# Second attention: column sides in turn for the value products, and forget-gate terms in bias tables

## The reference, cut to what matters

```python
def fox_mixer(cols, q_g, k_g, forget_bias):
    q = rms_norm(to_heads(cols['c_q'], FOX_HEADS), q_g)
    k = rms_norm(to_heads(cols['c_k'], FOX_HEADS), k_g)
    v = to_heads(cols['c_v'], FOX_HEADS)
    log_f = jax.nn.log_sigmoid((cols['c_f'] + forget_bias).astype(jnp.float32))
    c = jnp.cumsum(log_f, axis=1).transpose(0, 2, 1)
    ...
        logits = (jnp.einsum('bhqd,bhsd->bhqs', qi, k).astype(jnp.float32) * (HEAD_DIM ** -0.5)
                  + ci[..., None] - c[:, :, None, :])
        logits = jnp.where(t_pos[:, None] >= key_pos[None, :], logits, NEG_INF)
        probs = jax.nn.softmax(logits, axis=-1)
        return jnp.einsum('bhqs,bhsd->bhqd', probs.astype(v.dtype), v)
```

## Time and profile before

| | us |
|---|---|
| median of 3 runs | 2215.01 |
| the runs | 2211.79, 2215.01, 2215.42 |
| profiled execution, its span | 2214.5 |
| PE busy in it | 2169.7 (98%) |
| VectorE busy in it | 1212.5 (55%) |
| ScalarE busy in it | 519.1 (23%) |

### The profile page before, as it was taken

How to read it: one execution, slowest core, us unless ns; L and a number is a source line. 1 busy time by engine, 2 the same in 40 slices (tenths; PEclk the granted TensorE clock), 3 DMA queues, 4 the chain that set the end, 5 groups by cost and what they waited for, 6 DMA issues and landing times.

```text
span 2214.5 us, 40429 instructions
## 1 busy us (share of the span) xinstructions
PE 2169.7 (98%) x17748; PEld 1767.9 (80%) x17748; DVE 1212.5 (55%) x2285; ACT 519.1 (23%) x1103; POOL 159.8 (7%) x180
## 2 busy tenths in 40 slices
PE   8999899999999999999999999999999999999999
PEld 5854689994688888885666667899988877789999
DVE  4647744444545555755645554487544353228874
ACT  3224722221100000004434443100121143302100
POOL 0002132220000000000211221000010000000000
PEclk9999999999999999999999999999999799999999
DMA  7221022221322245323212221545454422144453
GB/s 314 96 76 57 20 80 80 80 80 39 111 80 95 79 190 226 116 101 138 86 58 76 76 77 58 190 172 180 172 183 160 152 77 96 66 153 146 169 174 132
DMA packets 38247, 260.70 MB, mean 118 GB/s; under 512 B 4647, under 2 KB 6327, under 8 KB 7480
## 3 DMA queue, kind: packets, MB, share of 16 engines
q1 hardware_dynamic: 34416, 248.83, 31.1%
q10 hardware_dynamic: 2760, 6.11, 0.7%
q0 software_dynamic: 896, 3.18, 0.4%
HBM read 256.49 MB, written 1.08 MB: 116 GB/s over the span
## 4 chain that ended last, share of the span: by engine, by line
PE 85%; DVE 3%; ACT 1%; issue 1%; POOL 0%; ACTq 0%; DVEq 0%; POOLq 0%
PE pairs L315 24%; PE bank L315 11%; PE pairs L1804 11%; PE pairs L185 11%; PE bank L1375 4%; PE pairs L1375 4%; PE pairs L2785 4%; PE pairs L1933 1%; PE bank L439 1%; PE pairs L2739 1%; PE bank L1907 1%; PE bank L453 1%; PE bank L1897 1%; PE bank L2719 1%; PE bank L1872 1%
## 5 line engine op out<-in xcount | busy, mean ns | idle before, releaser
L1804 PE MATMUL pairs<-h_sb,ring_sb 128*128 128x512 f32 (+1 forms) x784 | 263.9, 492 | 0.0
L1804 PEld LDWEIGHTS pairs<-h_sb,ring_sb 128*128 128x128 f32 x784 | 147.5, 190 | 105.3 <-issue 94.7
L185 PE MATMUL pairs<-h_sb,ring_sb 128*128 128x256 f32 (+1 forms) x720 | 223.4, 470 | 0.9 <-DVE h_sb L669 0.9
L185 PEld LDWEIGHTS pairs<-h_sb,ring_sb 128*128 128x128 f32 x720 | 136.9, 192 | 84.7 <-issue 72.3
L315 PE MATMUL pairs<-mid 128*128 128x128 f32 (+1 forms) x1304 | 197.3, 306 | 0.6 <-DVE mid L357 0.6
L315 PEld LDWEIGHTS pairs<-mid 128*128 128x128 f32 x1304 | 179.5, 192 | 11.2 <-issue 1.1
L335 DVE TENSOR_TENSOR mid<-ring_sb 128x512 f32<-128x512 f32 (+1 forms) x105 | 71.7, 683 | 123.7 <-DMA ring_sb<-weights 69.4
L315 PE MATMUL bank<-mid 128*128 128x256 f32 x544 | 122.7, 380 | 0.1
L315 PE MATMUL pairs<-h_sb,ring_sb 128*128 128x128 f32 (+1 forms) x784 | 118.2, 303 | 3.0 <-ACT h_sb L583 2.3
L185 PE MATMUL pairs<-big,ring_sb 128*128 128x256 f32 (+1 forms) x544 | 114.2, 376 | 0.5 <-DVE big L2848 0.5
L315 PEld LDWEIGHTS pairs<-h_sb,ring_sb 128*128 128x128 f32 x784 | 106.1, 194 | 10.3 <-ACT h_sb L583 2.7
(11 more groups left out here) (529 smaller groups left out, 3649.0 us busy)
## 6 DMA issues: line engine op xcount, KB each, us to landing
ring_sb<-weights SPq DMA_DIRECT2D x237, 1024.0 KB, 4.8
x_sb<-tokens ACTq DMA_DIRECT2D x1, 2048.0 KB, 12.1
mid<-bias_table POOLq DMA_DIRECT2D x1, 1536.0 KB, 9.0
const_table<-consts ACTq DMA_DIRECT2D x1, 1200.0 KB, 10.6
mid<-bias_table POOLq DMA_DIRECT2D x1, 1024.0 KB, 12.4
out<-x_sb ACTq DMA_DIRECT2D x4, 256.0 KB, 2.6
lora_w<-lora ACTq DMA_DIRECT2D x1, 512.0 KB, 14.0
vec_table<-vectors SPq DMA_DIRECT2D x1, 285.0 KB, 16.1
```

Of the source, the lines that this page charges most:

```text
L185: last = pe.matmul(out, w[:, k, c, :], rhs(j * kt + k), start=(j == 0 and k == 0), stop=(j * kt + k == k_end - 1))
L1804: ins = pe.matmul(m.pairs[:, at % 2, c, 0:T], w[:, k, c, :], m.h[:, k, TOK - T:TOK], start=(k == 0), stop=(k == 7))
```

## The change

Value products have the side as the inner loop now: each product of side 0 is followed by the same product of side 1. The fox scores are the query-key products alone, as in swa. For each fox head h there are two bias tables (in columns of `x` and `h` that are free by then), one for each query tile. They are built during earlier units: after the values of the units with chunk 0 to 7 (nsa1 and swa), PE broadcasts the row of `logf` of head h = chunk to all partitions, into the other half of that chunk's PSUM bank (`forget_row_pe`); VectorE adds to it the query's own sum, a column of `forget_tok`, and the causal mask (`forget_bias_dve`), before it copies the unit's heads out. `forget_tok` comes from two more small products in group 9 of the projection, which now waits for the second count of `gates_moved`, and one more copy on VectorE in group 11.

```diff
@@ -2383,8 +2383,10 @@
             v_turn_pe(s, m, g - 7)
         if g == 9:
             pe.wait_ge(sem["v_tokens"], s.next("v_tokens"))
-            pe.wait_ge(sem["gates_moved"], s.next("gates_moved"))
+            pe.wait_ge(sem["gates_moved"], s.next("gates_moved", 2))
             for tt in range(2):
+                pe.matmul(m.bank[:, 3, 8 * tt:8 * tt + 8], m.c2[CF, 28, tt * P:tt * P + P], m.const("ident")[CF, CF],
+                          start=True, stop=True)
                 ins = pe.transpose(m.bank[:, 2, 24 * tt:24 * tt + 24], m.gate_rows[:, tt * P:tt * P + P],
                                    m.const("ident")[0:24, 0:24])
             ins.then_inc(sem["gates_turned"], s.one("gates_turned"))
@@ -2598,14 +2600,15 @@
         .then_inc(sem["dve_step"], s.one("dve_step"))
     dve.wait_ge(sem["dve_step"], s.made("dve_step"))
     dve.tensor_scalar(m.logf[CF, 1, :], t, -1.0, None, ALU.mult)
-    dve.tensor_copy(backwards(z), by_tile(t)).then_inc(sem["dve_step"], s.one("dve_step"))
-    dve.wait_ge(sem["dve_step"], s.made("dve_step"))
+    dve.tensor_copy(backwards(z), by_tile(t)).then_inc(sem["gates_moved"], s.one("gates_moved"))
+    dve.wait_ge(sem["gates_moved"], s.made("gates_moved"))
     for g in range(NORM_FROM, IN2_GROUPS):
         squares_dve(s, m, g)
         if NORM_FROM < g < IN2_GROUPS - 1:
             normed_dve(s, m, g - 1)
         if g == 11:
             dve.wait_ge(sem["gates_turned"], s.next("gates_turned"))
+            dve.tensor_copy(m.forget_tok, m.bank[:, 3, 0:16])
             src = m.bank[:, 2, 0:48].rearrange("p (t h n) -> p t h n", t=2, n=3)
             for at, tt, n in ((0, 0, 1), (1, 0, 2), (2, 0, 0), (3, 1, 0), (4, 1, 1), (5, 1, 2)):
                 ins = dve.tensor_copy(m.gate_tok[:, :, at:at + 1], src[:, tt, :, n:n + 1])
@@ -2658,8 +2661,9 @@
         return [m.bias_nsa[:, h, 128:256]] * 2 + [m.bias_nsa[:, h, a:a + 16 * (N_CMP - 1) + 1:16] for a in at]
     if kind == "nsa1":
         return [m.bias_nsa[:, h, 0:256]] * 2
-    near = m.bias_swa[:, h, :] if kind == "swa" else m.fox_mask
-    return [near[:, 128:256], near[:, 0:256]]
+    if kind == "fox":
+        return [m.bias_fox0(h), m.bias_fox1(h)]
+    return [m.bias_swa[:, h, 128:256], m.bias_swa[:, h, 0:256]]
 
 
 def attention_scores_pe(s, m, t):
@@ -2693,18 +2697,9 @@
     for tt, a, b in ((0, 0, 128), (1, 128, 384)):
         for side, rows, out in sides:
             ins = pe.matmul(out[:, a:b], m.q2[rows, q, tt * P:tt * P + P], m.c2[rows, k, 0:b - a],
-                            start=True, stop=kind == "swa")
-            if kind == "swa" and tt:
+                            start=True, stop=True)
+            if tt:
                 ins.then_inc(sem["scores"], 1)
-        if kind == "fox":
-            for side, rows, out in sides:
-                h = head_of(kind, c, side)
-                sel = m.const("ident")[CF, 32 + h:33 + h]
-                pe.matmul(out[:, a:b], m.c2[CF, 28, tt * P:tt * P + P], sel.broadcast_to([8, b - a]),
-                          start=False, stop=False)
-                ins = pe.matmul(out[:, a:b], sel.broadcast_to([8, P]), m.logf[CF, 1, 0:b - a], start=False, stop=True)
-                if tt:
-                    ins.then_inc(sem["scores"], 1)
 
 
 def attention_turn_pe(s, m, t):
@@ -2728,31 +2723,53 @@
     pe.wait_ge(sem["turned_out"], m.base + 2 * (t + 1))
     if chunk >= 2 and kind != "nsa1":
         pe.wait_ge(sem["heads_out"], chunk - 1)
-    for side in range(2):
-        rows = slice(64 * side, 64 * side + 64)
-        out, w = m.pair4[rows, chunk % 2, 0:SEQ], m.turned2[t % 2][:, side, :]
-
-        def value(tt, v):
-            return m.vtok2[:, tt, v, rows]
-
-        def add(tt, v, n, start, stop, keys=P):
-            return pe.matmul(out[:, tt * P:tt * P + P], v, w[0:keys, n * P:n * P + P], start=start, stop=stop)
-
-        if kind == "nsa0":
-            add(0, value(0, 0), 0, True, False)
-            add(0, value(0, 1), 1, False, False)
-            cmp = m.vcmp[:, rows]
-            add(0, cmp, 2, False, True, N_CMP)
-            ins = add(1, cmp, 3, True, False, N_CMP)
-        elif kind == "nsa1":
-            for n in range(4):
-                ins = add(1, value(n % 2, n // 2), n, False, n == 3)
-        else:
-            v = 2 if kind == "swa" else 3 + c
-            add(0, value(0, v), 0, True, True)
-            add(1, value(0, v), 1, True, False)
-            ins = add(1, value(1, v), 2, False, True)
+
+    def add(tt, values, n, start, stop, keys=P):
+        for side in range(2):
+            rows = slice(64 * side, 64 * side + 64)
+            ins = pe.matmul(m.pair4[rows, chunk % 2, tt * P:tt * P + P], values[:, rows],
+                            m.turned2[t % 2][0:keys, side, n * P:n * P + P], start=start, stop=stop)
+        return ins
+
+    def value(tt, v):
+        return m.vtok2[:, tt, v, :]
+
+    if kind == "nsa0":
+        add(0, value(0, 0), 0, True, False)
+        add(0, value(0, 1), 1, False, False)
+        add(0, m.vcmp, 2, False, True, N_CMP)
+        ins = add(1, m.vcmp, 3, True, False, N_CMP)
+    elif kind == "nsa1":
+        for n in range(4):
+            ins = add(1, value(n % 2, n // 2), n, False, n == 3)
+    else:
+        v = 2 if kind == "swa" else 3 + c
+        add(0, value(0, v), 0, True, True)
+        add(1, value(0, v), 1, True, False)
+        ins = add(1, value(1, v), 2, False, True)
+    if kind != "nsa0" and forget_head(chunk) is not None:
+        ins = forget_row_pe(s, m, chunk)
     ins.then_inc(sem["weighted"], 1)
+
+
+def forget_head(chunk):
+
+    return chunk if chunk < 8 else None
+
+
+def forget_row_pe(s, m, chunk):
+
+    h = forget_head(chunk)
+    sel = m.const("ident")[CF, 32 + h:33 + h]
+    return s.eng.matmul(m.pair4[:, chunk % 2, SEQ:2 * SEQ], sel.broadcast_to([8, P]), m.logf[CF, 1, :], start=True, stop=True)
+
+
+def forget_bias_dve(s, m, chunk):
+
+    dve, h = s.eng, forget_head(chunk)
+    row, own = m.pair4[:, chunk % 2, SEQ:2 * SEQ], m.forget_tok
+    dve.scalar_tensor_tensor(m.bias_fox0(h), row[:, 0:P], own[:, h:h + 1], m.fox_mask[:, P:2 * P], ALU.add, ALU.add)
+    dve.scalar_tensor_tensor(m.bias_fox1(h), row, own[:, 8 + h:9 + h], m.fox_mask, ALU.add, ALU.add)
 
 
 def attention_pe(s, m):
@@ -2845,6 +2862,8 @@
         if t and ATTENDED[t - 1][0] != "nsa0":
             chunk = OUT_CHUNK[t - 1]
             dve.wait_ge(sem["weighted"], m.base + t)
+            if forget_head(chunk) is not None:
+                forget_bias_dve(s, m, chunk)
             dve.tensor_copy(backwards(m.o_fm[:, chunk, :]), by_tile(m.pair4[:, chunk % 2, 0:SEQ])) \
                 .then_inc(sem["heads_out"], 1)
         if t < N_ATTENDED:
@@ -3199,7 +3218,16 @@
         self.gate_tok = ph[:, 2008:2056].rearrange("p (h n) -> p h n", n=6)
         self.gain2 = ph[:, 2056:2075]
         self.gate_rows = ph[0:24, 2080:2336]
-
+        self.forget_tok = ph[:, 2340:2356]
+
+
+    def bias_fox0(self, h):
+
+        return self.x[:, 4 + h // 2, P * (h % 2):P * (h % 2) + P]
+
+    def bias_fox1(self, h):
+
+        return self.h[:, h, 0:SEQ]
 
     def conv_x(self, g):
```

## The result

The changed kernel takes 2193.01 us in the median of 4 runs (2191.98 to 2197.07), the kernel before 2214.77 (4 runs); the ratio is 0.9911, 95% interval 0.9896 to 0.9927, which is 16 to 23 us less. In a second measurement it was 2193.92 against 2214.41, ratio 0.9909 (0.9895 to 0.9923). The forecast was 2196.0, a ratio of 0.9914. By the ratio the gain is 19.7 us; the medians of these few runs lie 21.8 apart.

A forecast was written before the change was run, and what follows sets the result against it. PE in the second attention was taken to bound the kernel. Terms 12.8 + 8.2 + 3.4 - 5.0 - 0.4 = 19.0 us off; 2214.5 - 19.0 + 0.5 = 2196.0 us, range 2191.5 to 2203.

The forecast's parts named there:

- What bounds it: Second attention: PE is busy without a gap, so a microsecond off PE comes off the time unless another engine becomes late.
- Forget terms out of the scores: Scores of four forgetting units: 4.06 us each falls to 0.86 as in sliding-window units, 12.8 us off.
- Value products: Attention units: alternating sides all pair, saving 1.16 us per nsa0, 0.45 per nsa1, 0.22 per swa or fox; 8.2 off.
- The 3.9 us of loss: Value products: rival that alternating sides does not pair and today's partial overlap goes too; 2208.1 us in all, chance 0.06.
- Row products: After the values of eight nsa1 and swa units: one 8-row product each, 0.63 us with changeover, 5.0 us on.
- VectorE's builds: Two additions per head, 0.8 us, eight times, ahead of the heads' copy: hidden, 0 us, with 0.75 left in unit 2.
- Group 9: Projection: two products of 8 rows by 8 columns, four records at 0.108 us, beside two transposes; 0.4 us on.
- The clock: Forgetting units: with scores cut to 0.86 us, the half clock no longer appears; 3.4 us off.
- Both falls: Two drops of the granted clock to 0.50 after forgetting scores, 1.7 us each, expected gone; rival that they stay, chance 0.12.
- Sum: Whole kernel: 12.8 + 8.2 + 3.4 - 5.0 - 0.4 = 19.0 us off, giving 2196.0.

The follow-up runs named there:

- the run over 128 rows: Kernel before, with the forget products of the fox scores made over all 128 rows instead of 8, same sums; 2208.9 us against 2213.18, ratio 0.9983.

## Why the prediction was right, point by point

- **What bounds it.** It is PE in the attention, as read from the earlier trace rows: 19.86 us left the chain there, and the time fell by about as much. No other engine became late.
- **Forget terms out of the scores, 12.8.** 4.06 became 0.86 in four units, 12.8.
- **Value products, 8.2.** They gave 8.6: nsa0 1.14, nsa1 0.49, swa and fox 0.26 in each unit. The paired rate was right; the changeover was put at 0.20 where the value products show about 0.15. Records of line 2730 in flight agree with the pairing (x, as in the earlier trace rows): 6 of them, where one side alone had 3. Since the ends of matmul records are modelled, the time on the chain is the proof.

```profile
1791.20:1791.30 0.10, 0.10 (x6) 1.00 0.00 0
```

  The rule of the Trainium skill ("TensorE: Matmul & The Clock Gate", section "The mechanism" of Part 3), that a weight load overlaps matmuls in flight only with another row group, does not hold for these products: in nsa1, swa and fox both sides have all 128 rows and load 64 columns each, and they pair. The 3.9 us of loss that it would give is contradicted by 150.07 against 157.11.
- **Row products, 5.0.** 8 x 0.62 = 4.96, and 5.00 by taking them away.
- **VectorE's builds, hidden.** The two instructions by form, and the place in unit 2 with the least room:

```profile
L2772 DVE SCALAR_TENSOR_TENSOR h_sb<-pairs,const_table 128x256 f32<-128x256 f32 x8 | 3.8, 475 | 0.0
...
L2771 DVE SCALAR_TENSOR_TENSOR x_sb<-pairs,const_table 128x128 f32<-128x128 f32 x8 | 2.8, 351 | 27.7 <-PE pairs L2764 27.7
```

```profile
1792.59 0.35 DVE L2771 SCALAR_TENSOR_TENSOR x_sb<-pairs,const_table 128x128 f32<-128x128 f32 x1 [3.12 <-PE pairs L2764]
1792.85 0.48 DVE L2772 SCALAR_TENSOR_TENSOR h_sb<-pairs,const_table 128x256 f32<-128x256 f32 x1
...
1794.01 1.43 DVE L2883 TENSOR_SCALAR big<-big,small 128x128 f32<-128x128 f32 x8
```

```profile
1796.33 0.88 PE L2714 MATMUL bank<-const_table,big 128*128 128x128 f32 x6
```

  The two instructions take 0.351 and 0.475 us in the mean and lap over each other, so from the first start (1792.59) to the copy of the heads it is 0.65, not the 0.8 of the sum. Scaling ends at 1795.44, transposes start at 1796.33: 0.89 us to spare, where 0.75 was worked out.
- **Group 9, 0.4.** 0.53 instead of 0.23: 0.30, so the four records took less than the 0.108 each that were put for them.
- **The clock, 3.4.** Both falls are gone. The prediction tied them to the forgetting scores and did not say what in them does it; the run over 128 rows shows that in these units it is the few rows of the forget products.
- **Sum.** 12.8 + 8.6 + 3.4 - 4.96 = 19.84 in the attention, of 19.86 measured, less 0.30 in group 9: 19.6 against 19.0 forecast. The ratio gives 19.7, with an interval of 16 to 23, and the two profiled executions are 19.3 apart. The median after is 3.0 below the forecast; 0.6 of this is in the terms above, the rest is scatter that no term of the prediction stood for. Two profiles of the changed kernel begin the attention at 1771.24 and 1767.89 us, with the same attention behind.

## What to carry to other kernels

In this kernel a product cost PE its columns, whether it had 8 rows or 128 (0.43 us for two records of 256 columns either way), and a changeover of 0.15 to 0.2 us came on top in the places read here where the shape of the array changed. So look whether a broadcast or a rank-one term can go to an engine or a DMA queue with time to spare, into a table that an instruction reads anyway. Where two half-wide products go to different partitions, try writing them in turn: here 16 records took 1.02 us instead of 1.51. And when one term of a sum is to be read to a tenth of a us on a kernel whose runs scatter by several, measure between two fixed instructions of the trace, not end to end.

## What was not expected

The granted clock fell to 0.50 while PE was busy without a gap. With forget products of 8 rows, the kernel before had the half clock behind two of four forgetting units (1.7 us lost each time), and blocks of 3.65 us of 8-row products had it in or behind five of eight units, while the forget products over 128 rows left the clock at 1.00 over 42.7 us. Making them over all the rows was worth 3.9 us by itself, 3.4 of them by the clock.

Few rows are not all that goes with a fall, though. Ahead of the attention, in the projection, the kernel before does 128 records of 128 rows but only 30 columns from 1717.6 to 1741.4 us, and the clock is at 0.50 from 1721.5 to 1745.4, with PE busy all the time; here are these records in the timeline and one window of the stretch:

```profile
1717.60 23.81 PE L185 MATMUL pairs<-big,ring_sb 128*128 128x30 f32 x128
```

```profile
1728.31:1731.73 3.42, 3.42 (x18) 3.42 (x17) 0.00 (x0) 0.00 (x0) 0.00 (x0) 0.50 0.83 285
```

Every profile here has these 23.9 us, that of the run over 128 rows too. No run varies these records, so what they have in common with the 8-row products stays open.
